# Merging the high and low input halves into one 512-column product in the 256-token nets of a two-block transformer, and gates by Silu

## The reference

```
def swiglu_ffn(h, w_in, w_out):
    g, u = jnp.split(h @ w_in, 2, axis=-1)
    return (jax.nn.silu(g) * u) @ w_out
```

## Time and profile before

| | |
|---|---|
| median of 3 runs | 3101.33 us |
| the runs | 3100.0, 3101.33, 3105.69 us |
| the profiled execution, first to last instruction | 3099.1 us |
| TensorE busy | 3049.1 us, 98% |
| weight loads busy (beside the products) | 2726.2 us, 88% |
| VectorE busy | 2108.9 us, 68% |
| ScalarE busy | 1308.7 us, 42% |
| HBM read | 483.90 MB |

### The profile page before, as it was taken

One profiled execution on the slowest core, in us unless ns is written; L12 is line 12 of the kernel. 1 busy time (PEld: TensorE's weight loads), 2 busy tenths in 40 slices (PEclk: granted clock), 3 DMA queues, 4 the chain that ended last, 5 costly groups with the idle time before them and its releaser, 6 DMA issues.

```text
span 3099.1 us, 51504 instructions
## 1 busy us (share of the span) xinstructions
PE 3049.1 (98%) x21499; PEld 2726.2 (88%) x21499; DVE 2108.9 (68%) x3542; ACT 1308.7 (42%) x1983; POOL 2.3 (0%) x6
## 2 busy tenths in 40 slices
PE   8999999999999999999999999999999999999999
PEld 8999999999999999997888866788887888886999
DVE  6768767667778766667666487766655676567655
ACT  4455555455455555454222232532224222246544
POOL 0000000000000000000000000000000000000000
PEclk9999999999999999999999999999999999999999
DMA  7655445657655455656444365545444444350763
GB/s 212 179 171 182 150 155 172 190 171 211 190 171 177 150 167 176 181 174 202 148 142 142 109 181 172 147 129 150 129 130 142 143 138 147 109 163 28 218 177 109
DMA packets 677985, 490.64 MB, mean 158 GB/s; under 512 B 23167, under 2 KB 671737, under 8 KB 677753
## 3 DMA queue, kind: packets, MB, share of 16 engines
q1 hardware_dynamic: 675449, 482.69, 52.0%
q10 hardware_dynamic: 2304, 4.66, 0.5%
HBM read 483.90 MB, written 3.39 MB: 157 GB/s over the span
## 4 chain that ended last, share of the span: by engine, by line
PE 89%; DVE 5%; ACT 2%; DMA 2%; DVEq 1%; issue 1%; SPq 0%; ACTq 0%
PE ps L718 28%; PE ps L720 27%; PE ps L719 27%; DVE wl L1952 1%; PE ps L1253 1%; ACT wh L1445 1%; DVE Pp L1944 1%; PE ps L864 1%; DMA raw<-in_ada_w 1%; DVE XX L1944 0%; PE ps L1060 0%; PE ps L802 0%; PE ps L847 0%; DMA shifted<-u_rows 0%; DVE Hl L1944 0%
## 5 line engine op out<-in xcount | busy, mean ns | idle before, releaser
L1952 DVE TENSOR_TENSOR wl<-raw,wh 128x1024 fp32r<-128x1024 f32 (+2 forms) x780 | 921.7, 1185 | 683.9 <-ACT wh L1445 682.6
L1445 ACT ACTIVATE wh<-raw 128x1024 fp32r<-128x1024 f32 (+2 forms) x780 | 795.4, 1026 | 1385.4 <-PE ps L720 1353.4
L718 PE MATMUL ps<-Fh,wh 128*128 128x256 f32 (+1 forms) x3296 | 1001.2, 304 | 6.4 <-DVE Fl L2671 1.6
L719 PE MATMUL ps<-Fl,wh 128*128 128x256 f32 (+1 forms) x3296 | 995.4, 302 | 0.0
L720 PE MATMUL ps<-Fh,wl 128*128 128x256 f32 (+1 forms) x3296 | 995.4, 302 | 0.0
L718 PE MATMUL ps<-Hh,wh 128*128 128x256 f32 (+1 forms) x2576 | 868.5, 337 | 5.0 <-DVE Hl L1944 2.6
L719 PE MATMUL ps<-Hl,wh 128*128 128x256 f32 (+1 forms) x2576 | 856.5, 332 | 0.0
L720 PE MATMUL ps<-Hh,wl 128*128 128x256 f32 (+1 forms) x2576 | 856.2, 332 | 0.0
L718 PEld LDWEIGHTS ps<-Fh,wh 128*128 128x128 f32 x3296 | 629.7, 191 | 35.1 <-issue 5.1
L720 PEld LDWEIGHTS ps<-Fh,wl 128*128 128x128 f32 x3296 | 629.8, 191 | 23.4
L719 PEld LDWEIGHTS ps<-Fl,wh 128*128 128x128 f32 x3296 | 629.9, 191 | 22.7
(11 more groups left out here) (325 smaller groups left out, 2037.8 us busy)
## 6 DMA issues: line engine op xcount, KB each, us to landing
raw<-in_ffn_w_in SPq DMA_DIRECT2D x176, 512.0 KB, 5.1
raw<-in_ffn_wi SPq DMA_DIRECT2D x176, 512.0 KB, 5.2
raw<-in_ada_w SPq DMA_DIRECT2D x144, 512.0 KB, 4.5
raw<-in_w_in SPq DMA_DIRECT2D x112, 512.0 KB, 4.5
raw<-in_ffn_w_out SPq DMA_DIRECT2D x64, 512.0 KB, 4.0
raw<-in_ffn_wo SPq DMA_DIRECT2D x64, 512.0 KB, 4.6
raw<-in_ffn_w_out SPq DMA_DIRECT2D x32, 384.0 KB, 3.4
raw<-in_ffn_wo SPq DMA_DIRECT2D x32, 384.0 KB, 3.8
```

Of the source, the lines that this page charges most:

```text
L718: nc.tensor.matmul(o, wh[:, u.par, kc, w], xh(kc), start=(kc == 0), stop=False)
L719: nc.tensor.matmul(o, wh[:, u.par, kc, w], xl(kc), start=False, stop=False)
L1445: nc.scalar.activation(tile_of(wh[:, u.par], t, n), tile_of(raw[:, u.slot], t, n), ACT.Copy) \
L1952: V.tensor_tensor(tile_of(wl[:, u.par], t, n), tile_of(raw[:, u.slot], t, n), tile_of(wh[:, u.par], t, n).bitcast(F32), ALU.subtract).then ...
```

## The change

`HALVED` lists the gate units of the first four nets that are merged: in each group all but the last, and not the first of a net. `two_products` makes a product of wh with both input halves side by side (512 columns: tokens of Xh in the bank's first half, of Xl in its second), and one of wl with Xh (256 columns, added in the second half). So a bank's halves must be summed when read. `halves` runs such a unit, always tile 0 first and then tile 1. It is used for the gate units of `HALVED`, for the output units of all 256-token nets but the last of each net (`summed_late`), and for the first three units of the mixer's output. Hh and Hl, and Fh and Fl, become one buffer each (HH, FF), at the same places. ScalarE reads the second half to SBUF, VectorE adds the first and multiplies both tiles by r; the step to Fl of a merged unit moves behind the next unit's first low part (`product_low`). Output units add to x twice. Gates use Silu in all nets in place of (1 + tanh(g/2)) g, with the factors of the adds doubled in turn.

```
+def halved_gates():
+    out = []
+    for first in FFN_STARTS[:2 * DEPTH]:
+        k = first
+        for g, held in enumerate(GROUPS):
+            out += [k + i for i in range(held - 1) if (g, i) != (0, 0)]
+            k += held + 4
+    return {k: n + 1 for n, k in enumerate(out)}
...
+        def summed_late(n, g, kind, i):
+            return n == T and kind == "O" and (g, i) != (2, 3)
...
+            def two_products(u, x, kc, t, kc_n=C):
+                w = slice(P * t, P * t + P)
+                nc.tensor.matmul(two(bank(u, t)), wh[:, u.par, kc, w], x(kc), start=(kc == 0), stop=False,
+                                 skip_group_check=True)
+                return nc.tensor.matmul(bank(u, t, T), wl[:, u.par, kc, w], x(kc)[:, 0], start=False, stop=(kc == kc_n - 1),
+                                        skip_group_check=True)
+
+            def halves(u, x, kc_n=C, ready=None):
+                for t in range(2):
+                    pe.wait_ge(lo_done, u.lo_done(t))
+                    if t == 0:
+                        pe.wait_ge(banks_free[u.par], u.banks_free())
+                    for kc in range(kc_n):
+                        if ready is not None and t == 0:
+                            ready(kc)
+                        mm = two_products(u, x, kc, t, kc_n)
+                    mm.then_inc(mm_done, 1)
...
+                            elif u.k in HALVED:
+                                halves(u, both_parts(unscaled_both(norm), 1))
...
-                            linear(u, part(Fh, n), part(Fl, n), n, held, ready if i == 0 else None)
+                            if summed_late(n, g, kind, i):
+                                halves(u, both_parts(FF), held, ready if i == 0 else None)
+                            else:
+                                linear(u, part(Fh, n), part(Fl, n), n, held, ready if i == 0 else None)
...
-                    linear(Unit(k + M_WO + j), part(Hh, T, 1), part(Hl, T, 1), T, ready=m_ready if j == 0 else None)
+                    if j < 3:
+                        halves(Unit(k + M_WO + j), both_parts(HH, 1), ready=m_ready if j == 0 else None)
+                    else:
+                        linear(Unit(k + M_WO + j), part(Hh, T, 1), part(Hl, T, 1), T)
```

On ScalarE, in the gate unit of a net (behind `hi(u.later(2), 0)`); the one-column Tanh ahead of a net becomes a Silu:

```
+                        if u.k in HALVED:
+                            act.wait_ge(mm_done, u.mm_done(1))
+                            nc.scalar.activation(two(Tt[:, u.par, :]), low_pair(u), ACT.Copy).then_inc(lows_out, 1)
+                            hi(u.later(2), 1)
+                            act.wait_ge(a_done, fi * FC + g * 8 + (i + 1))
+                            nc.scalar.activation(Pp[:, u.par, T:2 * T], Tt[:, u.par, 0:T], ACT.Silu).then_inc(tanh_done, 1)
+                            act.wait_ge(prod_done, HALVED[u.k])
+                            nc.scalar.activation(Fh[:, 0, i, :], Pp[:, u.par, 0:T], ACT.Copy).then_inc(fh_done, 1)
+                            continue
                         if kind == "G" and norm is not None:
                             act.wait_ge(a_done, fi * FC + g * 8 + (i + 1))
-                            nc.scalar.activation(Tt[:, u.par, 0:n], Ss[:, 0:n], ACT.Tanh, scale=0.5).then_inc(tanh_done, 1)
+                            nc.scalar.activation(Tt[:, u.par, 0:n], Ss[:, 0:n], ACT.Silu).then_inc(tanh_done, 1)
```

On VectorE:

```
+                            if u.k in HALVED:
+                                lo(u.later(2), 0)
+                                if u.k - 1 in HALVED:
+                                    product_low(u.later(-1), i - 1, done + i)
+                                dve.wait_ge(lows_out, HALVED[u.k])
+                                both_sums = two(Tt[:, u.par, :])
+                                V.tensor_tensor(both_sums, pair(u), both_sums, ALU.add).then_inc(banks_free[u.par], 1)
+                                dve.drain()
+                                V.tensor_tensor(both_sums, both_sums, twice(r), ALU.mult).then_inc(a_done, 1)
+                                lo(u.later(2), 1)
+                                dve.wait_ge(tanh_done, done + (i + 1))
+                                V.tensor_tensor(Pp[:, u.par, 0:T], Pp[:, u.par, T:2 * T], Tt[:, u.par, T:2 * T], ALU.mult) \
+                                    .then_inc(prod_done, 1)
+                                continue
                             dve.wait_ge(mm_done, u.mm_done(0))
                             V.tensor_tensor(Ss[:, 0:n], bank(u, 0, n), r, ALU.mult).then_inc(a_done, 1)
                             lo(u.later(2), 0)
-                            done = fi * FC + g * 8
+                            if u.k - 1 in HALVED:
+                                product_low(u.later(-1), i - 1, done + i)
                             dve.wait_ge(tanh_done, done + (i + 1))
-                            stt(Ss[:, 0:n], Tt[:, u.par, 0:n], 1.0, Ss[:, 0:n], ALU.add, ALU.mult)
-                            dve.drain()
-                            V.tensor_tensor(Ss[:, 0:n], Ss[:, 0:n], r, ALU.mult)
+                            V.tensor_tensor(Ss[:, 0:n], Tt[:, u.par, 0:n], r, ALU.mult)
...
-                            stt(x, pair(u), 0.25, x, ALU.mult, ALU.add).then_inc(banks_free[u.par], 1)
+                            ins = stt(x, pair(u), 0.5, x, ALU.mult, ALU.add)
+                            if summed_late(n, g, kind, i):
+                                dve.drain()
+                                ins = stt(x, low_pair(u), 0.5, x, ALU.mult, ALU.add)
+                            ins.then_inc(banks_free[u.par], 1)
```

More of the change, by code:

```diff
@@ L275, in build @@
         Xx, Xc = XX[:, 0], XX[:, 1]
-        Hh = sb("Hh", [P, 2, C, T], F32R)
-        hh_ctx_at = off[0] - 4 * C * T
-        Hl = sb("Hl", [P, 2, C, T], F32R)
-        hl_ctx_at = off[0] - 4 * C * T
+        hh_ctx_at = off[0] + 4 * C * T
+        hl_ctx_at = off[0] + 3 * 4 * C * T
+        HH = sb("HH", [P, 2, 2, C, T], F32R)
+        Hh, Hl = HH[:, 0], HH[:, 1]
         edges = sb("edges", [P, 7 * P], at=hl_ctx_at)
         fh_at = off[0]
-        Fh = sb("Fh", [P, 2, C, T], F32R)
-        fl_at = off[0]
-        Fl = sb("Fl", [P, 2, C, T], F32R)
+        fl_at = off[0] + 4 * 2 * C * T
+        FF = sb("FF", [P, 2, 2, C, T], F32R)
+        Fh, Fl = FF[:, 0], FF[:, 1]
         decay = sb("decay", [P, C, T], at=fh_at)
@@ L489, in unscaled, with unscaled_both @@
             return (Hh, Hl) if norm % 4 == 3 else (Fh, Fl)
+        def unscaled_both(norm):
+            return HH if norm % 4 == 3 else FF
         def inverse_root(norm):
@@ L1457, in tanh_table, with silu_table @@
                 nc.scalar.activation(eps[:, 1:2], eps[:, 0:1], ACT.Tanh)
+            def silu_table():
+                nc.scalar.activation(eps[:, 1:2], eps[:, 0:1], ACT.Silu)
             def root_table():
@@ L1526, in deferred_norm @@
                         .then_inc(ctx_std, 1)
-                tanh_table()
+                if norm_i % 2 == 0:
+                    silu_table()
+                else:
+                    tanh_table()
                 act.wait_ge(rb_done, number(norm_i))
@@ L1551, in norm_parts @@
                 copy_modulation(BATCH_AT[after])
-                tanh_table()
+                if after in FFN_STARTS:
+                    silu_table()
+                else:
+                    tanh_table()
             def ffn(k, fi, n, after, norm=None):
@@ L1580, in ffn @@
                             nc.scalar.activation(tiny[:, 32:40], tiny[:, 40:48], ACT.Exp, scale=-1.0).then_inc(lam_exp, 1)
+                        if u.k in HALVED:
[7 more added lines that the diff above has]
+                            continue
                         if kind == "G" and norm is not None:
                             act.wait_ge(a_done, fi * FC + g * 8 + (i + 1))
[L1583 removed]
+                            nc.scalar.activation(Tt[:, u.par, 0:n], Ss[:, 0:n], ACT.Silu).then_inc(tanh_done, 1)
                         elif kind == "G":
                             act.wait_ge(mm_done, u.mm_done(0))
[L1586 to L1587 removed]
+                            nc.scalar.activation(Tt[:, u.par, 0:n], bank(u, 0, n), ACT.Silu).then_inc(tanh_done, 1)
                         if g == 2 and (kind, i) == ("O", 3):
@@ L2029, in gate_const @@
             def gate_const(l, i):
-                factor = 0.25 if i != 1 else (0.5 if l == 0 else 1.0)
+                factor = 1.0 if (l, i) == (1, 1) else 0.5
                 V.tensor_scalar(G1[:, i], MOD[:, l, (3 * i + 2) * C:(3 * i + 3) * C, :], factor, None, ALU.mult)
@@ L2136, in ffn @@
                             done = fi * FC + g * 8
-                            dve.wait_ge(tanh_done, done + (i + 1))
-                            stt(Ss[:, 0:n], Tt[:, u.par, 0:n], 1.0, bank(u, 0, n), ALU.add, ALU.mult)
-                            dve.drain()
                             if adding:
                                 add_modulation(*adding)
+                            dve.wait_ge(tanh_done, done + (i + 1))
                             dve.wait_ge(mm_done, u.mm_done(1))
```

(21 more changed lines are left out.)

9 lines of the change are left out of this document (7 added, 2 removed).

## The result

The changed kernel takes 3121.11 us (median of four runs, 3120.25 to 3123.40), the one before beside it 3100.89. The ratio is 1.0062, with a 95% interval of 1.0050 to 1.0074: slower, by more than twice the forecast's +8.4. The profiled execution has a span of 3118.5 us against 3099.1.

What follows compares the result with a forecast made beforehand. TensorE, busy 98% of the span, was taken as the bound. Terms -26.9 + 24.8 + 2.0 + 2.8 + 2.2 + 2.1 + 1.4 = +8.4 on 3101.3 gave 3109.7 us, range 3087 to 3120 (forecast's own 3103 to 3117).

Steps and rivals of the forecast that it cites:

- third rival: On TensorE: the merged product isn't cheaper, a triple staying near 0.36 us; 3122 us, or 3117; chance 0.12.
- Two of 256 cost 0.240, one of 512 costs 0.227: TensorE's gain: each merged pair saves about 0.013 us, over 2068 triples 26.9 us.
- triple: Three 256-column products on TensorE, 0.360 us; merged, one of 512 and one of 256 columns, forecast at 0.347 us.
- The boundaries of the first four nets: At three group ends per net, TensorE waits 2.35, 2.6 and 1.2 us for Fl: 24.8 us over four nets.
- squares: In the second layer's ffn2, ScalarE squares ctx inside merged units, lengthening the loop: 2.1 us.
- The loop of 5.82 us: VectorE and ScalarE wait on each other 5.82 us per merged gate unit; TensorE needs 5.55, so they lag 0.27 more each.
- The wait at the first output unit as lag plus early due time: After each group, tile-by-tile order needs the eighth chunk 2.27 us after the gate unit's end, before 5.04; lag adds waiting.
- The last net: With plain gate units, its three groups still wait 0.6, 0.6 and 0.8 us: 2.0 us.
- the mixer's output: Its first output unit loses the joint order and waits 1.4 us for its last input: 2.8 us for two layers.
- the ends of ffn1: Second adds in the last group delay the reciprocal TensorE waits for by 1.1 us: 2.2 us in all.
- second adds: Three merged output units per last group each add 0.77 us, 2.3 us in all, of which 1.2 is absorbed.
- Table loads: If Exp and Silu share no table, a 1.28 us load per layer delays a product by 0.7: 1.4 us.

Runs made afterwards that it cites:

- no loop: The changed kernel with ScalarE's Fh copy of a merged unit moved behind the next unit's first high part; tile-by-tile order kept: 3095.22 us, ratio 0.9980.
- Joint order: The changed kernel with merged output units behind a group's end, and the mixer's first, taking both tiles of a chunk together: 3095.52 us, ratio 0.9980.
- Silu only: The changed kernel with no merged unit, leaving only the gates by Silu and the new buffers: 3101.19 us, ratio 0.9998 to before.
- gates only: The changed kernel with merged gate units but plain output units, the mixer's included: 3093.35 us, ratio 0.9973 to before.
- the best version here: The changed kernel with joint tiles, later Fh copy, last groups' output units unmerged and width order alternated every second chunk: 3080.90 us, ratio 0.9935.

## Why the prediction was wrong

The direction was right and so was the mechanism of the waits; the size was 11 us short, and the time lay 1.1 us outside the range. That it lies near the third rival's 3122 is chance: that rival had units of 5.76 us and 13.6 us at the boundaries, and the trace shows 5.55 to 5.65 and 30.1. Step by step:

- **"Two of 256 cost 0.240, one of 512 costs 0.227", so a triple becomes 0.347: this is the step that failed.** Both distances come from rows of equal products. Mixed, a triple costs 0.351 on the mean, so merging saves 0.009 and not 0.013: -18.5 us, not -26.9. 0.347 does occur, in the shorter unit, but only 37 of 96 undisturbed full units have that length, the other 59 the longer one. This mis-sized term is 8.4 of the 11 us. The third rival named this cause ("the change between two lengths") and priced only its extreme. The Trainium skill's 2.5 ns (TensorE: Matmul & The Clock Gate, "Wait — 56ns, not 53.3ns?") would give 5.2 us for the whole gain; by the measured saving it is too low by more than three times where each product loads its own weights.
- **The boundaries of the first four nets: right, though one part was missing.** Forecast with squares and table loads 28.3, measured 30.1, of which the slow clock at two boundaries is 4.0: 1.55 us in the first net and 2.4 in the fourth, by the triples above. Without it 26.1 is left, 2.2 less than forecast. In the first layer's ffn2, which has nothing but the lag, the three groups cost 1.98, 2.18 and 1.03 where I had 2.35, 2.6 and 1.2; its units take 5.65, so each adds less lag. In the first net, with units of 5.55, the first group costs 2.38, as forecast. I had looked at the clock only as a row of nines and not asked what a wait of 2 or 3 us does to it.
- **The loop of 5.82 us: right**, 5.85; "no loop" has 5.55 with one step taken out.
- **The wait at the first output unit as lag plus early due time: right.** "Joint order" and "no loop" each take away one of the two, and with it 26 us.
- **The last net (+2.0), the mixer's output (+2.8), the ends of ffn1 (+2.2): right**, 1.9, 2.9 and 2.1. The argument that 1.2 us of the second adds is absorbed because the first tile ends early held too: the joint order undoes it, and the 1.1 us appear in every net.
- **Table loads (+1.4)**: the loads are there, but each delays a product by 0.15 us instead of 0.7, so 0.3 in all.
- **The start of the last net and the unit ahead of it, +1.0 and +3.6**: put at nothing, since "DMA loads are as many". They are, but TensorE waits 4.3 us for the load of in_ada_w there instead of 1.5, and its clock is 0.50 from 2909.3 to 2916.1 us, around that wait's end at 2910.1. The wait is 3.3 to 4.7 us, with one or two slow stretches of 3.4 us around its end, in the profile of every kernel with merged output units, and 1.5 to 1.6 with none in those without (before, Silu only, gates only). Why was not tried. In the sum it is hidden by the -3.8 us of the second block.

What stays open: why a merged unit has two lengths and what picks one. Only breaks change it, and alternating the order removes it; nothing here shows what in the array or in the weight loads does it.

## What to carry to other kernels

Price a mixed sequence of instructions from a mixed sequence: here the distance between starts in rows of equal ones was the lower end for the mix, and a term that carries the sum needs both ends. A change that makes work due earlier and one that makes its producer lag may each be free; look at what they do together, at the first consumer that needs all of the producer's output. Count two waits of TensorE close together, the second of 2 us, as possibly 1.6 to 2.4 us more, for the clock behind them: the best version here (0.9935) keeps the merged products and has no such waits at its group ends. And where terms of a sum that should be nothing cancel, look at each: here a wait of 4.3 us instead of 1.5 stood behind a remainder of some 0.2.

## What the runs showed of the hardware

- A merged unit takes 5.55 or 5.65 us (triples of 0.347, or of 0.350 with every third or so at 0.361), the same instructions and data shapes in both; with the order 512, 256, 256, 512 it takes 5.57 (5.62 where both tiles of a chunk are taken together).
- TensorE ran at 1.2 GHz for 3.4 or 6.8 us behind two waits close together at a group's end (0.4 to 3.0 and then 2.0 us between starts), at some and not at others: the same boundary has it in one kernel and not in another whose waits are as long within tenths of a microsecond. Each stretch of 3.4 us cost 1.55 to 1.65 us.
- Silu and Exp need a table load of 1.28 us between them, each way; Tanh and Exp in the kernel before need none. In ScalarE's spare time the load cost nothing, in the loop 0.15 us.
